# A hybrid attention and SSD layer on eight cores: the decay tiles of the SSD part made during attention and kept in DRAM

## What is computed

```
a_cs  = cumsum(dt * A)                       # within a chunk, per head
seg   = a_t[..., :, None] - a_t[..., None, :]
decay = exp(where(causal, seg, -inf))        # (b, chunk, group, head, L, S)
cb    = einsum('bclgn,bcsgn->bcgls', C, B)
m     = cb[:, :, :, None] * decay
y_diag = einsum('bcgrls,bcsgrp->bclgrp', m, X * dt)
```

## Time and profile before

| | |
|---|---|
| median of 3 runs | 1903.23 us (1896.35 to 1906.76) |
| profiled execution | 1899.2 us; span 1897.7 us on the slowest core, 1879.5 us on the fastest |
| granted clock by core | 0.988 to 0.993 |
| TensorE busy | 1797.5 us (95% of the span), 11590 matmuls |
| VectorE busy | 1128.1 us (59%) |
| ScalarE busy | 741.6 us (39%) |
| GpSimd busy | 595.6 us (31%) |
| chain that ended last | TensorE 71%, VectorE 11%, DMA 8%, issue 5%, ScalarE 3% |

### The profile page before, as it was taken

The page is one execution under the profiler, slowest core; times in us unless marked ns, Lnnn a source line. Parts: engine busy times, 40 slices in busy tenths (PEclk is TensorE's granted clock), DMA queues, the critical chain, the costliest instruction groups (busy, mean ns, idle before and its releaser), DMA issues.

```text
span 1897.7 us, 35295 instructions; the slowest of 8 cores (1879.5 to 1897.7 us)
## 1 busy us (share of the span) xinstructions
PE 1797.5 (95%) x11590; PEld 998.2 (53%) x11590; DVE 1128.1 (59%) x2273; ACT 741.6 (39%) x1818; POOL 595.6 (31%) x730
## 2 busy tenths in 40 slices
PE   5999899999999888999999999999999999999996
PEld 2444455455445455666566656666566654444443
DVE  0134222222222435888988898888989887565565
ACT  1123433433344464555555555555555550000000
POOL 3000000000000103666765666666765660000000
PEclk9999999999999899999999999999999999999999
DMA  9919054441901511463738264453766574444341
GB/s 145 149 22 137 17 90 68 66 84 39 128 17 34 110 37 48 89 115 81 127 81 130 70 113 89 95 113 81 129 162 118 151 236 162 164 146 159 122 134 55
DMA packets 165460, 195.31 MB, mean 103 GB/s; under 512 B 96984, under 2 KB 123768, under 8 KB 158464
## 3 DMA queue, kind: packets, MB, share of 16 engines
q1 hardware_dynamic: 145888, 125.91, 26.1%
q0 software_dynamic: 19392, 67.15, 23.1%
HBM read 213.46 MB, written 42.22 MB: 135 GB/s over the span
## 4 chain that ended last, share of the span: by engine, by line
PE 71%; DVE 11%; DMA 8%; issue 5%; ACT 3%; POOL 1%; SPq 1%; DVEq 0%; ACTq 0%; POOLq 0%
PE bank L347 70%; DMA attst<-atg 3%; DMA vz_slab<-wpack 2%; DVE carry_r L363 2%; DMA slab<-wpack 2%; DVE cv_r L373 1%; DVE MT_r L363 1%; ACT tt L359 1%; ACT P L359 1%; DVE nrw_r L373 1%; DVE yn_r L373 1%; DVE t_r L363 1%; SPq L111 1%; DVE ss_r L368 1%; DVE carry_r L373 1%
## 5 line engine op out<-in xcount | busy, mean ns | idle before, releaser
L347 PE MATMUL bank<-xT_bf,slab 128*128 128x512 bf16 x2048 | 484.5, 382 | 20.6 <-DMA xT_bf<-xT 20.3
L347 PEld LDWEIGHTS bank<-xT_bf,slab 128*128 128x128 bf16 x2048 | 197.2, 99 | 233.2 <-issue 28.8
L347 PE MATMUL bank<-vz_slab,xT_bf 128*128 128x512 bf16 x1024 | 246.8, 384 | 9.2 <-DVE gz L373 6.7
L347 PE MATMUL bank<-w_out_bf,mb 128*128 128x512 bf16 x1024 | 234.7, 382 | 0.0
L347 PE MATMUL bank<-xT_bf,slab_r 128*128 128x512 bf16 x1024 | 234.1, 379 | 0.0
L359 ACT ACTIVATE dec_r<-abc_r,nb_tok 128x128 bf16<-128x128 f32 x512 | 204.7, 400 | 35.7 <-ACT dec_r L359 0.4
L363 POOL TENSOR_TENSOR t_r<-t_r,xd_r 128x256 f32<-128x256 f32 x120 | 102.4, 853 | 276.2 <-DVE t_r L363 274.1
L347 PEld LDWEIGHTS bank<-w_out_bf,mb 128*128 128x128 bf16 x1024 | 100.7, 99 | 122.1 <-issue 5.9
L363 POOL TENSOR_TENSOR abc_r<-abc_r,mask 128x512 f32<-128x512 f32 x128 | 159.8, 1249 | 9.0 <-DMA abc_r<-acs_d 8.4
L347 PEld LDWEIGHTS bank<-vz_slab,xT_bf 128*128 128x128 bf16 x1024 | 98.8, 99 | 116.8 <-issue 16.7
L347 PEld LDWEIGHTS bank<-xT_bf,slab_r 128*128 128x128 bf16 x1024 | 98.1, 98 | 106.7
(11 more groups left out here) (137 smaller groups left out, 2700.5 us busy)
## 6 DMA issues: line engine op xcount, KB each, us to landing
abc_r<-acs_d SPq DMA_DIRECT2D x128, 256.0 KB, 4.1
slab<-wpack POOLq DMA_DIRECT2D x20, 1024.0 KB, 12.7
xt<-x_tok SPq DMA_DIRECT2D x16, 1024.0 KB, 6.2
out<-xt SPq DMA_DIRECT2D x64, 256.0 KB, 2.3
wob<-w_out POOLq DMA_DIRECT2D x24, 512.0 KB, 25.0
slab_r<-wpack POOLq DMA_DIRECT2D x12, 1024.0 KB, 13.6
mb<-mixs SPq DMA_DIRECT2D x16, 768.0 KB, 5.2
xT_bf<-xT POOLq DMA_DIRECT2D x16, 512.0 KB, 44.6
```

The source lines that it names most:

```text
L347: return p.op("pe", lambda e: e.matmul(outap, lhsT, rhs, start=start, stop=stop), reads, writes, signal)
```

## The change

The decay tiles are made in the attention loop, from step 62 on, 107 of them by step 240 and the other 21 by step 312, and stored in DRAM as bf16 (`dec_d`, 128 KB each). For a tile m: `dec_load` (the same broadcast load as before, on SP, into one of three buffers dq), `dec_add` (GpSimd adds the mask, then VectorE adds nb_tok, broadcast over each head's 128 columns), `dec_exp` (one exponential of 512 columns on ScalarE, to bf16) and `dec_store` (SP). In one `dec_step`, placed behind `E_act(i)`, tile m is exponentiated and stored, m + 3 loaded and m + 1 added to. In the SSD stage `load_dec` fetches a finished tile four chunks ahead into one of four buffers; `load_abc`, `mask_abc` and the four exponentials are gone, and so is their wait. All evacuations into uT are on ScalarE. For room, the constants trade places, ones_bf is written by a memset at step 256 and attst has two buffers, not three.

```diff
-        attst = [mem.alloc([128, 512], BF16, "attst%d" % i) for i in range(3)]
+        attst = [mem.alloc([128, 512], BF16, "attst%d" % i) for i in range(2)]
...
-        def load_abc(i):
+        def load_dec(i):
             if i < 128:
-                p.dma("sp", [(abc[i % 4][:, :], acs_d[i // 16, i % 16].rearrange("h l -> (h l)")
-                              .unsqueeze(0).to_broadcast([128, 512]))], "abc%d" % (i % 4),
-                      reads=[b_acsd], writes=[b_abc[i % 4]])
-
-        def mask_abc(i):
+                p.dma("sp", [(dec_bf[i % 4][:, :], dec_d[i])], "dec%d" % (i % 4), reads=[b_decd[i]],
+                      writes=[b_dec[i % 4]])
+
+        def dq_of(i):
+            return i % 3 if i % 3 < 2 or i < DQ_TURN else 3
+
+        def dec_load(i):
             if i < 128:
-                TT("pool", abc[i % 4][:, :], abc[i % 4][:, :], mask4_bf[:, :], ALU.add, [b_const], [b_abc[i % 4]])
+                k = dq_of(i)
+                p.dma("sp", [(dq[k][:, :], acs_d[i // 16, i % 16].rearrange("h l -> (h l)")
+                              .unsqueeze(0).to_broadcast([128, 512]))], "dq%d" % k, reads=[b_acsd], writes=[b_dq[k]])
+
+        def dec_add(i):
+            if i < 128:
+                k, g, c = dq_of(i), i // 16, i % 16
+                v = dq[k][:, :].rearrange("p (a b) -> p a b", a=4)
+                TT("pool", dq[k][:, :], dq[k][:, :], mask4_bf[:, :], ALU.add, [b_const], [b_dq[k]])
+                TT("dve", v, v, nb_tok[:, c, 4 * g:4 * g + 4].unsqueeze(2).to_broadcast([128, 4, 128]), ALU.add,
+                   [b_ssdc], [b_dq[k]])
+
+        def dec_exp(i):
+            k, o_ = dq_of(i), dec_out(i)
+            ACT(dqo[o_][:, :], dq[k][:, :], AF.Exp, [b_dq[k]], [b_dqo[o_]])
+
+        def dec_store(i):
+            o_ = dec_out(i)
+            p.dma("sp", [(dec_d[i], dqo[o_][:, :])], "dqs%d" % o_, reads=[b_dqo[o_]], writes=[b_decd[i]])
...
-                CPY("dve" if j % 2 == 0 else "act", uT[:, j, 3:515], banks[bk][:, :], [bkb[bk]], [b_uT[j]])
+                CPY("act", uT[:, j, 3:515], banks[bk][:, :], [bkb[bk]], [b_uT[j]])
...
-            for hl in range(4):
-                ACT(dec_bf[i2][:, hl * 128:(hl + 1) * 128], abc[i3][:, hl * 128:(hl + 1) * 128], AF.Exp,
-                    [b_abc[i3], b_ssdc], [b_dec[i2]], bias=nb_tok[:, c, 4 * g + hl:4 * g + hl + 1])
...
+        DQ_START, DQ_LAST = 62, 107
+        DQ_TURN = DQ_LAST + 4
+        ndq = [0]
+
+        def dec_step(i):
+            if i < DQ_START:
+                return
+            if i == DQ_START:
...
+                for k in range(3):
+                    dec_load(k)
+                dec_add(0)
+            goal = (i - DQ_START) * DQ_LAST // (240 - DQ_START) if i < 240 else DQ_LAST + (i - 240) * (128 - DQ_LAST) // 72
+            while ndq[0] < min(128, goal):
+                m = ndq[0]
+                ndq[0] += 1
+                dec_exp(m)
+                dec_store(m)
+                dec_load(m + 3)
+                dec_add(m + 1)
...
             E_act(i)
             if i % 2 == 1 and i < 60:
                 next(dtgen, None)
+            dec_step(i)
...
-                load_abc(n + 5)
-                mask_abc(n + 3)
+                load_dec(n + 4)
```

More of the change, by code:

```diff
@@ L329, in build_program @@
     b_acsd = Buf("acs_d")
+    dec_d = nc.dram_tensor("dec_d", [128, 128, 512], BF16, kind="Internal").ap()
+    b_decd = [Buf("dec_d%d" % i) for i in range(128)]
     tot_d = nc.dram_tensor("tot_d", [32, 16], F32, kind="Internal").ap()
@@ L398, in build_program @@
     b_const = Buf("const")
+    b_const2 = Buf("const2")
     offs_of = mem.offs
@@ L560, in build_program @@
     load_xq(3)
-    p.dma("pool", [(mask4_bf[:, :], cp("mask4")), (ones_bf[:, :], cp("ones")),
+    p.dma("pool", [(mask4_bf[:, :], cp("mask4")),
                    (selA_bf[:, :, :].rearrange("p a b -> p (a b)"), cp("selAneg"))], "constb2", writes=[b_const])
@@ L732, in build_program @@
         atg = [mem.alloc([128, 4, 128], BF16, "atg%d" % i) for i in range(2)]
-        attst = [mem.alloc([128, 512], BF16, "attst%d" % i) for i in range(3)]
+        attst = [mem.alloc([128, 512], BF16, "attst%d" % i) for i in range(2)]
+        dq = [nc.alloc_sbuf_tensor_at("dq0", [128, 512], F32, offset=offs_of["dt_tok"]),
+              mem.alloc([128, 512], F32, "dq1"),
+              nc.alloc_sbuf_tensor_at("dq2", [128, 512], F32, offset=offs_of["ident_f"])]
+        dqo = [nc.alloc_sbuf_tensor_at("dqo%d" % i, [128, 512], BF16, offset=offs_of["tt%d" % i] + 1024)
+               for i in range(2)]
+        b_dqo = [Buf("dqo%d" % i) for i in range(4)]
+        b_dq = [Buf("dq%d" % i) for i in range(3)]
         b_P = [Buf("P%d" % i) for i in range(3)]; b_acc = [Buf("acc%d" % i) for i in range(2)]
         b_rv = [Buf("rv%d" % i) for i in range(2)]; b_atg = [Buf("atg%d" % i) for i in range(2)]
-        b_att = [Buf("att%d" % i) for i in range(3)]
-        inherit(b_gz[1:] + b_vp[1:] + b_P + b_acc + b_rv + b_atg + b_att, start_bufs)
+        b_att = [Buf("att%d" % i) for i in range(2)]
+        inherit(b_dq[1:2] + b_gz[1:] + b_vp[1:] + b_P + b_acc + b_rv + b_atg + b_att, start_bufs)
         p.op("dve", lambda e: e.memset(vp[1][:, :, :, 128:130], 2.0), [], [b_vp[1]])
@@ L765, in build_program @@
         gz_tok = [RB.alloc([128, 4, 256], BF16, "gz_tok%d" % i) for i in range(2)]
-        abc = [RE.alloc([128, 512], F32, "abc%d" % i) for i in range(4)]
+        dec_bf = [RE.alloc([128, 512], BF16, "dec%d" % i) for i in range(4)]
+        dq.append(RE.alloc([128, 512], F32, "dq3"))
+        dqo += [RE.alloc([128, 512], BF16, "dqo%d" % i) for i in (2, 3)]
+        b_dq.append(Buf("dq3"))
         normw = [RA.alloc([128, 256], F32, "normw0"), RD1.alloc([128, 256], F32, "normw1")]
@@ L782, in build_program @@
         cb_bf = [RA2.alloc([128, 128], BF16, "cb_bf%d" % i) for i in range(2)]
-        dec_bf = [RA2.alloc([128, 512], BF16, "dec%d" % i) for i in range(2)]
         MT_bf = [RA2.alloc([128, 512], BF16, "MT%d" % i) for i in range(2)]
@@ L1326, in O_st @@
         def O_st(h, g):
-            a3 = (4 * h + g) % 3
+            a3 = (4 * h + g) % 2
             bm = Buf("mix")
@@ L1350, in build_program @@
                     inherit(b_slab[2:4], b_vz4)
-                    inherit(b_abc, [b_q[2], b_k[2]])
+                    inherit(b_dec + b_dq[3:4] + b_dqo[2:4], [b_q[2], b_k[2]])
+                    inherit(b_tt, b_dqo[0:2])
                     load_seq(0)
@@ L1365, in build_program @@
                 p.dma("pool", [(wob[:, kb_, :], w_v[:, kb_, :])], "wob%d" % kb_, writes=[b_wob[kb_]])
+            if i == 256:
+                assert ndq[0] >= DQ_TURN
+                inherit([b_const2], b_dq[2:3])
+                p.op("dve", lambda e: e.memset(ones_bf[:, :], 1.0), [], [b_const2])
             if i >= 240 and i % 80 in (8, 24, 56):
@@ L1384, in build_program @@
                 front_mid(1)
-                load_abc(4)
             if gen is not None:
@@ L1399, in build_program @@
         in_att[0] = False
+        while ndq[0] < 128:
+            m = ndq[0]
+            ndq[0] += 1
+            dec_exp(m)
+            dec_store(m)
+            dec_load(m + 3)
+            dec_add(m + 1)
         start_gen(1)
```

30 lines of the change are left out of this document (15 added, 15 removed).

## The result

The changed kernel took 1918.8, 1927.2 and 1929.6 us (a fourth execution, at 2155 us with one die at a lower clock, 0.86, is left out), against a median of 1901 us before: 1.0125 times as long, 95% interval 1.0073 to 1.0177. **It is slower by 1.25%**, where 1889 us was forecast. The slower rival had 1927 us.

The account below looks back on a forecast made before the run. TensorE and VectorE were taken to be full in the SSD stage. 1899.2 - 22 (SSD) + 2 (pairs) + 6 (last pair) = 1885.2, or 1889 us as a median of runs; 8 in 10 range 1867 to 1926.

Parts of the forecast that it names:

- The slower rival: Attention pairs: half of 107 loads land in 8.6 us, past 6.3, costing 40 us; 1927 us in all, chance 0.22.
- What bounds the kernel: In the SSD stage TensorE (783.4 of 800 us) and VectorE (712.5 us) were both taken to be full.
- The reserve of 27 us in the SSD stage: The most this stage can give back: 26.52 us per four chunks against 25.67 undisturbed.
- The 1.33 us of a stall: SSD stage: TensorE's wait per group for VectorE's copy of u, 7 x 1.33 = 9 us, forecast to go.
- SSD stage, -22: SSD stage: with ten per cent of VectorE free, TensorE's waits shrink, saving 22 us, bounds -9 and -27.
- the unnamed 7 us: SSD stage: the last 7 us of the reserve, which no wait in the profile names; a third was forecast to return.
- Pairs, +2: Attention pairs: 7 us gained from thinner bursts, 9 us lost to late loads; +2 us, bounds -7 and +40.
- the 7 us of the bursts are gone: Attention pairs: GpSimd can't run ahead, wob copies go out singly, and the bursts' cost of 7 us disappears.
- 9 us new: Attention pairs: cost of late tile loads, two slab loads at 1.5 us, vz_slab's load at 5, odd ones 1.
- the three load buffers with their 6.3 us: Attention pairs: the tile chain, three tiles due every 9.75 us, holds while a load lands within 6.3 us.
- Last pair, +6: Last pair: 21 half-exposed exponentials +6, tile loads beside weight loads +3, eight exponentials gone -3; bounds -3 and +15.
- The weights: Chances over the whole kernel: forecast 0.50, slower rival 0.22, no change 0.16, better 0.12.

Follow-up runs that it names:

- e3: The changed kernel without the tiles' broadcast loads and without 127 of their 128 stores in attention, engine work kept; ratio to before 0.985.
- e14: The changed kernel with all tile loads and stores kept, but without the additions and exponentials between them; ratio to before 1.007.
- e9: The changed kernel with w_out copies moved to SSD half-groups without slab loads, and all 128 tiles made by step 240; ratio to before 1.020.
- e11: The changed kernel with the tile loads issued from ScalarE's queue instead of SP's; ratio to before 1.021.
- e15: The changed kernel with the 32 DMA transposes of atg replaced by plain copies; ratio to before 1.011.
- e17: The kernel before with u's evacuations and a three-column copy on ScalarE, and two Newton steps instead of three; 1877 to 1879 us, 0.988 of before.
- e8: The changed kernel with the w_out copies moved to the SSD stage, in the half of each group without slab loads; ratio to before 1.013.
- e4: The changed kernel with the w_out copies moved to the SSD stage, one after every fourth chunk; 1912 to 1923 us, 1.010 of before.

## Why the prediction was wrong, point by point

**What bounds the kernel: right.** The reserve of 27 us in the SSD stage was there; the changed kernel took 28 on its slowest core and 30 at the median. The 1.33 us of a stall, and the 4 us behind 26 waits, can be read from before's timeline: the group after the stall starts at 1024.74 us and is drawn 1.02 us long, though the next matmul starts at 1025.61; that one is drawn 0.38 us long, and the one after it starts at 1025.82. The drawn ends lie 0.15 and 0.17 us past the next start, and so much of an idle gap isn't seen: 1.16 + 0.17 = 1.33, and 26 x 0.17 = 4.4.

**SSD stage, -22: right in its mechanism, 8 short.** I had given the unnamed 7 us only a third. Beforehand I split the relief of VectorE wrongly. MT got no faster on average, 861 ns before and 864 after, and only its longest ones went; the carry product (766 to 445 ns), yn (613 to 485) and the taps (1023 to 878) did. A median far over the minimum was not a sign that the removed neighbour caused it. The sum came out low, 40 us of relief where there were 76: about 0.6 us for each of the 128 masks, where my share came to 0.3 us and the mask addition itself takes 1.16 us.

**Pairs, +2: this step failed**, at two terms. First, "the 7 us of the bursts are gone": the wob copies did go out one by one, and the longest transpose of the pairs fell from 35.0 to 15.1 us, as forecast (the 37.1 us that I read as a transpose is a store of attst to mixs in the same view), but GB/s in the stage rose from 59 to 159. Second, "9 us new" for the loads that come late: measured are 27 us of idle TensorE and 7 us of longer busy time at the lower clock. The sum had weighed each burst by one chain, the three load buffers with their 6.3 us. It left out that an exponential also waits for a store to land, with two output buffers: that was the 12.5 us above, and 28.2 us of ScalarE's waits in the pairs. And it had the other number that mattered and didn't price it: a DMA share near 0.86 forecast, 0.74 measured. With the transfers left out (e3) step 240 came back to 627.9 us; with the tile traffic kept and the copies of w_out gone, to 633.1 and 639.0. How much of the 35 us is the chain's and how much would be paid by others without it stays open, since e14 also brought the bursts back.

**Last pair, +6: wrong by 14.** The engine work costs 7 us (e3) where 6 less 3 were forecast. The transfers cost the other 13, sized at +3; without tiles in it (e9) the pair still takes 102 us.

**The slower rival named the result** (1927 forecast, 40 us in the pairs), and its bound of +40 held the measured 38. Its mechanism is only half right. Landings past 6.3 us are what TensorE waited behind in the trace, but they were a few very late ones, not half of all loads at 8.6 us: the median landing is 4.4. Its argument from one queue for transposes and loads was refuted as what makes them long: the longest took 15.9 to 19.8 us from another queue (e11), and 16.2 to 19.8 us with no transpose in theirs (e15).

**The weights were wrong.** I priced the gain from a stage where the resource was idle and the cost from transfers of 4.1 us, taken at a share of 0.56 in a stage that has 26 us of lead for them. In attention the lead is a quarter of that, 6.3 us.

What stays open: why tile traffic costs 0.80 to 0.86 us per MB there, whether each burst's length or the number of transfers in it is what counts (no run changed one without the other), what would be left with no wait for tiles and the copies apart, and e9's further 13 us up to step 240.

## What to carry to other kernels

Moving work to a stage where the compute engines are idle moves its transfers too (here 42 MB, which cost 35 us up to step 240); price them by the stage's DMA share and by the lead that a transfer has there, not by the landing they had elsewhere. When an engine near saturation holds the one that bounds the kernel, taking small work off it in place (e17: 58 us) can be worth nearly as much as moving a large piece away (SSD stage 819.4 against 813.6 us), and costs no traffic. A run that takes out one wait also lets the engine that waited run ahead (e14: eight copies of w_out at once, from 485.5 us on): before reading it as a test of the wait, look at what that engine now issues earlier.

## What the runs showed of the hardware

- The added time was roughly proportional to bytes at a DMA share under 1: +12, +22 and +35 us for 14, 28 and 42 MB while the share over 300 to 600 us on core 0 stood at 0.48, 0.66 and 0.76. Taking 17 copies of 512 KB out again brought back 24 to 30 us, at a share of 0.65 and 0.62 on the same core (e8, e4).
- Beside one casting load of 2 MB, itself 19.2 us long, a plain store of 128 KB took 17.4 us and a tile load 17.5 us; their medians in the pairs are 3.2 and 4.4 us. Behind a slab load and eight copies of w_out (e14) a transpose took 45.9 us. Issued from ScalarE's queue instead of SP's, the longest loads took 15.9 to 19.8 us.
- The 10 us with most of a stop of 10.5 us had a granted clock of 0.72 and the next 10 us one of 0.77, where before had 1.00 in both; over the last pair of the changed kernel it was 0.87 against 0.91. The 7 us of longer busy time in the pairs go with a clock of 0.96 instead of 0.99 there.
- The product MT kept its mean of about 0.86 us (0.415 at best) when a quarter of GpSimd's work beside it went away (from 66% of the stage to 48%), while its longest fell from 1.382 to 0.974 us and the carry product's mean from 766 to 445 ns.
